# A hybrid encoder layer on one core: paired stick-breaking scores with masks on TensorE, later projection chunks, and sample memory attention in four column groups

## The chip, the cores and the metric

The kernel runs on one core of a Trainium2 chip. The metric is the device time of one execution in microseconds (us), the median of several runs. The engines are named as the profile names them: PE is TensorE (PEld its weight loads), DVE VectorE, ACT ScalarE, POOL GpSimd, SP the engine that issues most transfers.

## What is computed

One layer of a streaming encoder with the same weights for a prompt of 1024 frames and for 8 samples of 16 frames with 512 cached frames each. Model width 1024. Cut to what the change touches:

```python
def mla_attend(...):                    # 8 heads: latent keys, softmax over visible chunks
    ...
def stick_breaking_attend(q, k, v, q_pos, k_pos):      # 4 heads of 64
    z = jnp.einsum('bqhd,bkhd->bhqk', q, k) * SB_SCALE
    before = (k_pos[None, :] < q_pos[:, None])[None, None]
    log_beta = jax.nn.log_sigmoid(z)
    log_keep = jnp.where(before, jax.nn.log_sigmoid(-z), 0.0)
    between = lax.cumsum(log_keep, axis=3, reverse=True) - log_keep
    a = jnp.where(before, jnp.exp(log_beta + between), 0.0)
    return jnp.einsum('bhqk,bkhd->bqhd', a, v)

def memory_attend(x, mem_k, mem_v, g, w_q, w_o):       # 4 heads of 128, 256 memory tokens
    q = (rmsnorm(x, g) @ w_q).reshape(B, T, MEM_HEADS, MEM_HD)
    p = jax.nn.softmax(jnp.einsum('bqhd,bkhd->bhqk', q, mem_k) * MEM_SCALE, axis=-1)
    return jnp.einsum('bhqk,bkhd->bqhd', p, mem_v).reshape(B, T, -1) @ w_o

z = rmsnorm(x) @ w_in                   # split into MLA, retention and stick-breaking parts
mixed = concat([o_mla, ret_y, o_sb]);  x = x + mixed @ w_out
x = x + memory_attend(x, mem_k, mem_v, ...)            # each sample has its own mem_k, mem_v
x = x + conv_ffn(x, ...)                # up-projection, causal conv, SwiGLU, down-projection
```

The prompt's memory keys and values come from mem_prompt, each sample's from a cache.

## The kernel before

Activations lie feature-major: 128 features on the partitions, T = 1152 frames (1024 of the prompt, then 8 x 16 of the samples) in the free dimension. The matrices of weights are multiplied in three fp32r products (high part by high part, high by low, low by high), 128x384 each: one output block of 128 features is NCH = 3 chunks of 384 frames (split_products, L1864). POOL splits each 512 KB slot of weights into w_hi and w_lo (L813, L816). Attention works in f32, in which PE makes two passes of each matmul (two records in the profile).

In order of time the kernel has: input projection and retention (to about 300 us), one hand-written pipeline for stick-breaking and prompt MLA (to 640), sample MLA, the output projection W_OUT, memory queries, memory attention with its output (841 to 970), and the FFN (to the end).

**The pipeline of steps.** STEPS is a table. Five packs of query tiles, PACKS = (7), (6,0), (5,1), (4,2), (3), each of at most 1024 key columns per head, make one pass of two heads. Ten "sb" steps (t = 0 to 9, the first with tile 3) do the four stick-breaking heads of the prompt. Then come four pairs of prompt MLA heads of five "mla" steps each, with four "sbs" steps (sample stick-breaking, two samples each) among them. For each step t and head hh PE makes scores (scores, L2080; sample_scores, L2103) into the PSUM banks S[hh], then the transposes of step t-1 (L2129), then values of step t-2 (L2152). For sb steps DVE adds the mask `hide` to the diagonal blocks (sb_mask, L1509), ACT takes two sigmoids (sb_sigmoids, L986 and L987), DVE does a scan and a product (L1536, L1541), and ACT copies the transposed probabilities (probT, L1015). The two heads of an sb step lie on partitions 0 to 63 and 64 to 127 of z. For mla steps DVE takes the row maximum, ACT the exp (L1004), DVE the normalisation (L1552).

**Projection chunks.** STEP_CHUNKS (L270) says after which head of which step one of 11 chunks of the next MLA pair's q, k, v and absorbed q ("a") is projected (project_chunk, L2170 to L2182). PE puts it in bank 7. DVE evacuates q chunks (q_pass, L1575), ACT k, v and a chunks (L1059 to L1072). For the first pair they begin at step 2, two per step.

**Memory attention.** A loop over n = 0 to N_MEM+1 has eight prompt tiles (n = 0 to 7) and four pairs of samples (n = 8 to 11). PE makes scores of n, values of n-2 and transposes of n-1. For a pair of samples the scores use a 128-column weight qm_pair in which a sample's and head's 16 frames stand at their place among zeros, built by eight small ACT copies per pair (L1205): eight matmuls add up in one bank (L2329). Values take mv_c as weight and 16 columns of m_probT as moving operand, 16 matmuls per pair (sample_values, L2300), woven between the products of one of four early chunks of the memory output (memory_output, L2285). The other 20 of 24 chunks follow the loop, block by block; DVE adds each to x (L1737) and then does, per block m, the sums and split for the FFN's norm (residual, L1668, L1672, with ACT's square and rounding, L1158, L1159). x is reloaded by SP from x_mid in four transfers (L774). mk_c and mv_c are the samples' memory caches.

What releases whom is written by hand as semaphores; the functions that the change touches:

## Time and profile before

| | |
|---|---|
| median of 3 runs | 1822.57 us (1821.88 to 1822.60) |
| profiled execution | 1819.94 us |
| its span, first to last instruction | 1818.2 us |
| mean granted clock of PE | 0.985 |
| PE busy | 1760.5 us, 97% of the span |
| PEld busy | 1609.5 us, 89% |
| DVE busy | 1085.4 us, 60% |
| ACT busy | 538.9 us, 30% |
| POOL busy | 493.7 us, 27% |

The page gives, for the slowest core, each engine's busy time, the chain of work that ended last (followed back from the last instruction, at each step to what released it), the costliest groups, and the transfers. Windows give busy times in a stretch with the granted TensorE clock as a share of full speed: 1.00 is 2.4 GHz, 0.50 is 1.2 GHz. In a timeline, x6 at the end means six records in a row, and [3.80 <-DVE q_pass L1575] an idle time before them and what ended it. A matmul's end is modelled: the time to the next start is what counts in a stream.

### The profile page before, as it was taken

How to read it: one execution, taken by the hardware profiler on the slowest of the kernel's cores; microseconds unless marked ns; L12 is line 12 of the kernel's file. 1: busy time of each engine (PE TensorE's matmuls, PEld its weight loads, DVE VectorE, ACT ScalarE, POOL GpSimd, SP SyncE). 2: the span in 40 equal slices, each digit the busy share in tenths (PEclk: the TensorE clock that was granted, in tenths of full speed). 3: DMA queues.
4: the chain of work that ended last, by engine and by line, in shares of the span. 5: the costliest groups of instructions: out<-in, count | busy, mean ns of one | idle time of the engine just before them, and what ended most of it. 6: DMA issues, size and time to landing. Idle time of an engine off the chain costs nothing.

```text
span 1818.2 us, 26442 instructions
## 1 busy us (share of the span) xinstructions
PE 1760.5 (97%) x10471; PEld 1609.5 (89%) x10471; DVE 1085.4 (60%) x1459; ACT 538.9 (30%) x977; POOL 493.7 (27%) x219
## 2 busy tenths in 40 slices
PE   7999999899999999999999999999999999999997
PEld 7998799565666659998999999999999999999987
DVE  7864466676555745545446765655656556565667
ACT  6211211566555533112323312112121130211234
POOL 1771121000000102432023443333333433333331
PEclk9999999899999999999979999999999999999999
DMA  5230110411111402423321111111111111111112
GB/s 216 82 104 31 62 44 16 128 45 47 59 47 48 157 12 89 151 74 147 126 84 36 47 37 45 46 35 46 46 35 46 38 43 46 38 42 46 36 43 105
DMA packets 34973, 119.28 MB, mean 66 GB/s; under 512 B 4944, under 2 KB 7984, under 8 KB 32464
## 3 DMA queue, kind: packets, MB, share of 16 engines
q1 hardware_dynamic: 32592, 108.76, 18.5%
q10 hardware_dynamic: 2304, 9.44, 1.5%
q8 instruction: 56, 0.92, 0.2%
q14 instruction: 21, 0.17, 0.0%
HBM read 100.73 MB, written 15.17 MB: 64 GB/s over the span
## 4 chain that ended last, share of the span: by engine, by line
PE 89%; DVE 5%; ACT 2%; issue 2%; SPq 1%; DMA 1%; ACTq 0%; DVEq 0%
PE scores L1864 34%; PE bank L1864 32%; PE scores L2099 3%; PE bank L2129 2%; PE scores L1944 2%; PE bank L2152 2%; PE bank L2170 2%; PE scores L1888 1%; DVE kbuf L1536 1%; PE bank L2146 1%; PE bank L1875 1%; PE scores L2096 1%; PE scores L2329 1%; PE scores L2112 1%; PE bank L2300 1%
## 5 line engine op out<-in xcount | busy, mean ns | idle before, releaser
L813 POOL TENSOR_TENSOR w_hi<-w_raw,zero 128x1024 fp32r<-128x1024 f32 x96 | 188.9, 1968 | 1246.7 <-PE bank L1864 568.9
L1864 PE MATMUL scores<-act_hi,w_hi 128*128 128x384 f32 x960 | 324.2, 338 | 0.0
L1864 PE MATMUL scores<-act_hi,w_lo 128*128 128x384 f32 x960 | 322.6, 336 | 0.0
L1864 PE MATMUL scores<-act_lo,w_hi 128*128 128x384 f32 x960 | 322.6, 336 | 0.0
L816 POOL TENSOR_TENSOR w_lo<-w_raw,w_hi 128x1024 fp32r<-128x1024 f32 x96 | 251.2, 2617 | 7.6
L1792 DVE TENSOR_TENSOR x<-bank,x 128x384 f32<-128x384 f32 x216 | 120.4, 558 | 103.6 <-PE bank L1864 103.6
L1864 PEld LDWEIGHTS scores<-act_hi,w_hi 128*128 128x128 f32 x960 | 180.5, 188 | 0.6 <-issue 0.2
L1864 PEld LDWEIGHTS scores<-act_lo,w_hi 128*128 128x128 f32 x960 | 180.5, 188 | 0.3 <-issue 0.2
L1864 PEld LDWEIGHTS scores<-act_hi,w_lo 128*128 128x128 f32 x960 | 180.5, 188 | 0.0
L1864 PE MATMUL bank<-act_hi,w_hi 128*128 128x384 f32 x528 | 177.9, 337 | 0.0
L1864 PE MATMUL bank<-act_hi,w_lo 128*128 128x384 f32 x528 | 177.4, 336 | 0.0
L1864 PE MATMUL bank<-act_lo,w_hi 128*128 128x384 f32 x528 | 177.4, 336 | 0.0
L1766 DVE SCALAR_TENSOR_TENSOR conv<-ext,consts,conv 128x1168 f32<-128x1168 f32 x44 | 117.6, 2672 | 79.4 <-ACT conv L1231 79.4
L1864 PE MATMUL bank<-s_hi,w_hi 128*128 128x384 f32 (+2 forms) x454 | 153.0, 337 | 0.0
L1864 PE MATMUL bank<-s_lo,w_hi 128*128 128x384 f32 (+2 forms) x454 | 152.7, 336 | 0.0
L1864 PE MATMUL bank<-s_hi,w_lo 128*128 128x384 f32 (+2 forms) x454 | 152.6, 336 | 0.0
L1242 ACT ACTIVATE s_hi<-conv 128x1024 fp32r<-128x1024 f32 x20 | 21.2, 1060 | 344.1 <-DVE conv L1775 344.1
L1864 PEld LDWEIGHTS bank<-act_hi,w_hi 128*128 128x128 f32 x528 | 99.3, 188 | 1.0 <-issue 0.8
L1864 PEld LDWEIGHTS bank<-act_lo,w_hi 128*128 128x128 f32 x528 | 99.3, 188 | 0.0
L1864 PEld LDWEIGHTS bank<-act_hi,w_lo 128*128 128x128 f32 x528 | 99.3, 188 | 0.0
L1768 DVE SCALAR_TENSOR_TENSOR conv<-ext,consts,conv 128x1168 f32<-128x1168 f32 x44 | 84.3, 1916 | 5.7 <-DVE conv L1766 3.0
L1864 PEld LDWEIGHTS bank<-s_hi,w_hi 128*128 128x128 f32 x454 | 85.4, 188 | 0.4
(341 smaller groups left out, 3298.6 us busy)
## 6 DMA issues: line engine op xcount, KB each, us to landing
w_raw<-wstream SPq DMA_DIRECT2D x108, 512.0 KB, 3.6
x_blk<-xT ACTq DMA_DIRECT2D x8, 576.0 KB, 4.6
x_mid<-x_blk ACTq DMA_DIRECT2D x8, 576.0 KB, 3.1
x<-x_mid SPq DMA_DIRECT2D x4, 1152.0 KB, 7.8
z<-cache_k SPq DMA_DIRECT2D x4, 1024.0 KB, 5.3
z<-cache_v SPq DMA_DIRECT2D x4, 1024.0 KB, 7.3
mk_c<-mk_c SPq DMA_DIRECT2D x4, 1024.0 KB, 11.5
mv_c<-mv_c SPq DMA_DIRECT2D x4, 1024.0 KB, 13.5
```

What stands on the lines that cost most here:

```text
L813: pool.tensor_tensor(w_hi[:, k], w_raw[:, k], zero[:].unsqueeze(2).to_broadcast([P, KB, P]), ALU.add).then_inc(w_rounded, 1)
L816: pool.tensor_tensor(w_lo[:, k], w_raw[:, k], w_hi[:, k].bitcast(F32), ALU.subtract).then_inc(w_split, 1)
L1242: act.activation(dst[:, 0:TP], conv[:, 0, 0:TP], ACT.Copy)
L1766: own_v(dve.scalar_tensor_tensor(c, ext[:, ab, 1:EXT - 1], conv_tap(m + NFF * ab, 1), c, ALU.mult, ALU.add))
L1768: dve.scalar_tensor_tensor(c, ext[:, ab, 2:EXT], conv_tap(m + NFF * ab, 2), c, ALU.mult, ALU.add).then_inc(conv_done, 1)
L1792: dve.tensor_tensor(x[:, m, frames(c)], bank[6 + q % 2][:, 0:CH], x[:, m, frames(c)], ALU.add).then_inc(d_evac, 1)
L1864: mm = pe.matmul(out, w[:, k, at + kb], x(kb), start=first and kb == 0 and n == 0, stop=last and kb == n_kb - 1 and n == 2)
L1944: mm = pe.matmul(bank[c][:, 0:CH], w[:, 0, kb], x[:, kb, frames(c)], start=i == 0 and n == 0, stop=i == KB - 1 and n == 2)
L2099: mm = pe.matmul(S[hh][:, at:end], q_pass[i % 2][:, hh, tile(j)], k_pass[i % 2][:, hh, keys], start=True, stop=True)
L2129: mm = pe.transpose(bank[4 + g % 2][:, tile(b)], taken(t, hh)[:, tile(4 * k + b)], ident[:])
L2152: mm = pe.matmul(bank[6][64 * hh:64 * hh + 64, tile(n)], v, probT[:, t % 2, hh, at + P * b:at + P * b + P], start=b == 0, stop=b == j)
L2170: mm = pe.matmul(bank[7][:, 0:CH], w_pass[:, s, (2 * hh + kb) * P:(2 * hh + kb + 1) * P], z[:, Z_CQ + kb, frames(k)], start=kb == 0, stop= ...
```

## The change

- **Stick-breaking scores.** sb_scores(t) makes both heads' scores, piece by piece alternating head 0 (rows 0 to 63) and head 1 (rows 64 to 127), after both heads' previous sigmoids. After each tile PE adds the mask to the diagonal block of each head, as ident times hide accumulated in the bank. sb_mask on DVE is gone; ACT's sigmoids wait for s_ready and run ahead of the copies of probT. PE's order in an sb step is: scores of both heads, transposes of head 0, chunk, values, transposes of head 1, chunk.
- **Chunks of the first pair** follow the table FIRST_CHUNKS, from step 3 to step 9.
- **MLA.** A pair's first scores wait for the last k chunk, its first values for the last v chunk. ACT evacuates the chunk after head 1 before that head's exp.
- **sample_scores** alternates the two 64-column groups, f outside.
- **POOL** waits for the last prompt normalisation before it splits the W_OUT slots.
- **Sample memory attention.** Weights have 32 columns, head h writes partitions 32h to 32h+31 (scores into S[n%2], values into bank 6, with mv_c as moving operand of 128 columns). ACT copies the raw values (m_raw), PE turns them with two transposes into bank 7, ACT rounds and DVE splits. qm_pair is built once, at n = 4, by two ACT operations.
- **Memory output.** Seven chunks (MO_EARLY) are made inside the loop, at n = 8 to 14, in two banks, and DVE adds them there. The order of the 24 is new, with the third chunks of blocks 0 to 3 after the first two of each. SP issues the reloads of x in another order and earlier.

The diff, cut:

```diff
-MO_CHUNKS = [(0, 1), (1, 0), (0, 0), (1, 1)]
-MO_CHUNKS += [(m, c) for m in range(KB) for c in range(NCH) if (m, c) not in MO_CHUNKS]
+MO_CHUNKS = [(0, 0), (1, 0), (0, 1), (1, 1), (2, 0), (2, 1), (3, 0), (3, 1)] + [(m, 2) for m in range(4)]
+MO_CHUNKS += [(m, c) for m in range(4, KB) for c in range(NCH)]
+MO_EARLY = 7
+
+MO_BANKS = [(1, 3)[d % 2] if d < 8 else 3 * (m % 2) + c for d, (m, c) in enumerate(MO_CHUNKS)]
...
+FIRST_CHUNKS = ((3, 0), (3, 1), (4, 0), (4, 1), (5, 0), (5, 1), (6, 0), (6, 1), (7, 0), (9, 0), (9, 1))
+LAST_KEYS, LAST_VALUES = CHUNKS.index(("k", 1)), CHUNKS.index(("v", 1))
 STEP_CHUNKS = [[[], [], []] for _ in range(N_STEPS + 2)]
 for _n in range(NCK):
-    STEP_CHUNKS[2 + _n // 2][_n % 2 + 1].append((0, _n))
+    STEP_CHUNKS[FIRST_CHUNKS[_n][0]][FIRST_CHUNKS[_n][1]].append((0, _n))
...
-            for n in range(4):
-                if n < 2:
-                    sp.wait_ge(ms_ready, N_MEM)
-                else:
-                    sp.wait_ge(m_pv, N_MEM)
+            for n, through, count in ((0, ms_ready, NTILE), (1, qm_pair_ready, 1), (3, ms_ready, N_MEM),
+                                      (2, m_turned, DB // 2)):
+                if n == 0:
+                    sp.wait_ge(qm_pair_ready, 1)
+                sp.wait_ge(through, count)
                 sp.dma_start(x[:, 2 * n:2 * n + 2], io["x_mid"][:, 2 * n:2 * n + 2]).then_inc(x_in_again[n], 16)
...
+            pool.wait_ge(p_ready, N_ITEMS)
+            with pool.Fori(W_OUT // 2, NW // 2 - 1) as i:
...
             def sb_sigmoids(t, hh):
...
-                act.wait_ge(sb_masked, RANK[t][hh] + 1)
+                act.wait_ge(s_ready, ITEM[t][hh] + 1)
...
+                    if kind == "sb":
+                        sb_sigmoids(t, hh)
                     if 1 <= t <= N_STEPS and hh < n_heads(t - 1):
                         copy_groups(t - 1, hh)
-                    if t < N_STEPS and hh < n_heads(t):
-                        kind = STEPS[t][0]
-                        sb_sigmoids(t, hh) if kind == "sb" else sample_sigmoids(t) if kind == "sbs" else mla_exp(t, hh)
-                    for chunk in STEP_CHUNKS[t][hh]:
-                        evacuate_chunk(*chunk)
+                    if hh:
+                        for chunk in STEP_CHUNKS[t][1]:
+                            evacuate_chunk(*chunk)
+                    if kind == "mla":
+                        mla_exp(t, hh)
+                    elif kind == "sbs" and hh == 0:
+                        sample_sigmoids(t)
+                    if hh == 0:
+                        for chunk in STEP_CHUNKS[t][0]:
+                            evacuate_chunk(*chunk)
...
+                if NTILE <= n - 2 < N_MEM:
+                    c = n - 2
+                    act.wait_ge(m_pv, c + 1)
+                    if c >= NTILE + 2:
+                        act.wait_ge(m_turned, c - NTILE - 1)
+                    act.activation(m_raw(c), bank[6][:, 0:256], ACT.Copy).then_inc(m_raw_copied, 1)
...
-            def sb_mask(t, hh):
...
+                if n - 3 >= NTILE:
+                    split_output(n - 3)
+                if 0 <= n - NTILE < MO_EARLY:
+                    memory_residual(n - NTILE)
+
+            for d in range(MO_EARLY, len(MO_CHUNKS)):
+                memory_residual(d)
+                m, c = MO_CHUNKS[d]
+                if c == NCH - 1:
+                    residual(m, 2 * KB, x[:, m], "g_ffn")
...
+            def sb_scores(t):
+
+
+                _, i, tiles = STEPS[t]
+                for hh in range(2):
+                    if PREVIOUS[t][hh] is not None:
+                        pe.wait_ge(exp_done, PREVIOUS[t][hh] + 1)
+                for j, first, width in spans(t):
+                    for at, end in pieces(first, width):
+                        for hh in range(2):
+                            rows = slice(64 * hh, 64 * hh + 64)
+                            pe.matmul(S[hh][:, at:end], z[rows, Z_SQ + i, tile(j)],
+                                      z[rows, Z_SK + i, at - first:end - first], start=True, stop=True)
+                    for hh in range(2):
+                        mm = pe.matmul(S[hh][:, first + width - P:first + width], ident[:], hide[:], start=False, stop=True,
+                                       skip_group_check=True)
+                        if j == tiles[-1]:
+                            mm.then_inc(s_ready, 1)
...
-                for bb in range(2):
-                    rows = slice(64 * bb, 64 * bb + 64)
-                    for f in range(2):
-                        pe.matmul(S[0][rows, 0:PAST], sb_rows[:, 2 * p + bb, f], cache_k[:, bb, f], start=f == 0,
-                                  stop=f == 1)
...
+                for f in range(2):
+                    for bb in range(2):
+                        pe.matmul(S[0][64 * bb:64 * bb + 64, 0:PAST], sb_rows[:, 2 * p + bb, f], cache_k[:, bb, f],
+                                  start=f == 0, stop=f == 1)
...
+            for t in range(2, N_SB):
+                sb_scores(t)
+                transposes(t - 1, 0)
+                for chunk in STEP_CHUNKS[t][0]:
+                    project_chunk(*chunk)
+                values(t - 2)
+                transposes(t - 1, 1)
+                for chunk in STEP_CHUNKS[t][1]:
+                    project_chunk(*chunk)
...
+            def sample_memory_scores(n):
...
+                for bb in range(2):
+                    for h in range(GH):
+                        mm = pe.matmul(S[n % 2][32 * h:32 * h + 32, 0:MEM], qm_pair[:, p, bb, h], mk_c[:, p, bb, h],
+                                       start=bb == 0, stop=bb == 1)
+                mm.then_inc(ms_ready, 1)
+
+            def sample_memory_values(c):
...
+                for bb in range(2):
+                    for k in range(2):
+                        for h in range(GH):
+                            mm = pe.matmul(bank[6][32 * h:32 * h + 32, tile(bb)],
+                                           m_probT[:, 2 * (c % 2) + k, 32 * h:32 * h + 32],
+                                           mv_c[:, p, bb, k, tile(h)], start=k == 0, stop=k == 1)
+                mm.then_inc(m_pv, 1)
+
+            def turn_memory_values(c):
+                pe.wait_ge(m_raw_copied, c - NTILE + 1)
+                pe.wait_ge(om_split, c)
+                for bb in range(2):
+                    mm = pe.transpose(bank[7][:, tile(bb)], m_raw(c)[:, tile(bb)], ident[:])
+                mm.then_inc(m_turned, 1)
...
+                if n - 3 >= NTILE:
+                    turn_memory_values(n - 3)
+                if 0 <= n - NTILE < MO_EARLY:
+                    memory_output(n - NTILE)
+                if 2 <= n < N_MEM + 2:
```

Where instructions now stand. PE, the scores of step 3 (tiles 5 and 1; scores0 and scores1 are the banks of head 0 and head 1, z holds queries and keys, prob the probabilities of step 2), before:

```order
L2096 MATMUL scores0<-z_66 128x512
L2096 MATMUL scores0<-z_66 128x256 x2
L2129 MATMUL bank4<-ident_53,prob_93 128x128 x4
L2129 MATMUL bank5<-ident_53,prob_93 128x128 x4
L2096 MATMUL scores1<-z_66 128x512
L2096 MATMUL scores1<-z_66 128x256 x2
L2129 MATMUL bank4<-ident_53,prob_93 128x128 x4
L2129 MATMUL bank5<-ident_53,prob_93 128x128 x4
L2170 MATMUL bank7<-z_66,w_pass_108 128x384 x2
```

And after, from the second piece of tile 5 on:

```order
L2162 MATMUL scores0<-z_66 128x256
L2162 MATMUL scores1<-z_66 128x256
L2165 MATMUL scores0<-hide_110,ident_53 128x128
L2165 MATMUL scores1<-hide_110,ident_53 128x128
L2162 MATMUL scores0<-z_66 128x256
L2162 MATMUL scores1<-z_66 128x256
L2165 MATMUL scores0<-hide_110,ident_53 128x128
L2165 MATMUL scores1<-hide_110,ident_53 128x128
L2196 MATMUL bank4<-ident_53,prob_93 128x128 x4
L2196 MATMUL bank5<-ident_53,prob_93 128x128 x4
L2239 MATMUL bank7<-z_66,w_pass_108 128x384 x2
L2221 MATMUL bank6<-probT_100,sv_tok_76 64x128 x16
```

Both heads' scores now stand ahead of all transposes, the two heads' matmuls alternate, a mask follows each tile, and the second head's transposes stand behind the values.

PE in the memory loop, n = 10 (mk_c and mv_c are the samples' caches, om_hi and om_lo the attention output, split), before:

```order
L2329 MATMUL scores0<-mk_c_139,qm_pair_138 128x256 x8
L1864 MATMUL scores0<-om_hi_134,w_hi_50 128x384
L2300 MATMUL bank6<-m_probT_137,mv_c_140 128x16 x2
L1864 MATMUL scores0<-om_lo_135,w_hi_50 128x384
L2300 MATMUL bank6<-m_probT_137,mv_c_140 128x16 x2
```

And after, from the end of n = 9 to the scores of n = 11:

```order
L2449 MATMUL bank4<-ident_53,m_prob_136 128x128
L2449 MATMUL bank5<-ident_53,m_prob_136 128x128
L2380 MATMUL scores0<-mk_c_139,qm_pair_138 32x256 x8
L1918 MATMUL scores0<-om_hi_134,w_hi_50 128x384
L1918 MATMUL scores0<-om_lo_135,w_hi_50 128x384
L1918 MATMUL scores0<-om_hi_134,w_lo_51 128x384
```

On PE then come the other nine products of this chunk, and behind them, up to the chunk of n = 11:

```order
L2394 MATMUL bank6<-mv_c_140,m_probT_137 32x128 x16
L2449 MATMUL bank4<-ident_53,m_prob_136 128x128
L2449 MATMUL bank5<-ident_53,m_prob_136 128x128
L2380 MATMUL scores1<-mk_c_139,qm_pair_138 32x256 x8
L2403 MATMUL bank7<-ident_53,m_probT_137 128x128 x2
```

The values stand in one piece behind a whole output chunk instead of between its products, and the two turning transposes are new.

## Rows read from the trace of the kernel before

**Rows 1.** The page's chain that ended last, shares of the span by engine.
```profile
PE 89%; DVE 5%; ACT 2%; issue 2%; SPq 1%; DMA 1%; ACTq 0%; DVEq 0%
```

**Rows 2.** Windows: us, busy us (instructions) of each engine, TensorE clock, DMA share, GB/s.
```profile
340.50:357.50 17.00, 16.47 (x40) 9.20 (x42) 10.45 (x14) 7.24 (x10) 0.00 (x0) 0.50 0.01 3
360.00:410.00 50.00, 47.70 (x334) 31.64 (x334) 37.87 (x46) 35.70 (x64) 0.00 (x0) 1.00 0.16 41
637.40:640.90 3.50, 3.13 (x24) 2.81 (x26) 2.83 (x8) 1.79 (x5) 0.00 (x0) 0.51 0.36 130
...
910.50:931.00 20.50, 19.84 (x76) 19.02 (x77) 1.78 (x5) 0.72 (x3) 0.00 (x0) 0.50 0.18 65
```

**Rows 3.** Timeline of PE: start, us, engine, line, operation, passes, idle before.
```profile
341.03 2.08 PE L2173 MATMUL bank<-z,w_pass 128*128 128x512 f32 x2 [3.80 <-DVE q_pass L1575]
...
418.86 1.55 PE L2099 MATMUL scores<-k_pass,q_pass 128*128 128x512 f32 x3
```

**Rows 4.** Timeline of step 7, PE and ACT.
```profile
395.40 1.09 PE L2129 MATMUL bank<-ident,prob 128*128 128x128 f32 x8
...
396.43 1.99 PE L2096 MATMUL scores<-z 64*128 64x512 f32 x6
...
397.07 1.03 ACT L986 ACTIVATE kbuf<-scores 128x1024 f32<-128x1024 f32 x1
...
399.04 1.08 ACT L1015 ACTIVATE probT<-bank 128x512 f32<-128x512 f32 x2
...
400.00 1.97 PE L2152 MATMUL bank<-probT,sv_tok 128*64 128x128 f32 x32
```

**Rows 5.** Timeline of PE, step 0.
```profile
298.67 1.13 PE L2096 MATMUL scores<-z 64*128 64x512 f32 x4
```

**Rows 6.** Timeline of PE, retention.
```profile
160.07 0.49 PE L2035 MATMUL bank<-q_dec,state 128*128 128x128 f32 x2
160.49 0.44 PE L2032 MATMUL bank<-kept,rv_tok 128*64 128x128 f32 x4
```

**Rows 7.** Waits of PE from 418 to 625: us in total, times, longest.
```profile
PE bank L2170 <- ACT k_pass L1060: 4.3, 3, 1.4
```

**Rows 8.** Timeline of PE, the first sample stick-breaking step.
```profile
449.34 1.93 PE L2112 MATMUL scores<-z,sb_rows 128*64 128x512 f32 x4
...
451.12 0.64 PE L2112 MATMUL scores<-z,sb_rows 128*64 128x512 f32 x1
451.22 0.49 PE L2115 MATMUL scores<-z,sb_rows 128*64 128x128 f32 x3
...
453.41 0.76 PE L2129 MATMUL bank<-ident,prob 128*128 128x128 f32 x5
```

**Rows 9.** Timeline of DVE and POOL in prompt MLA.
```profile
434.99 0.88 DVE L1552 TENSOR_SCALAR prob<-prob,row_sum 128x896 f32<-128x896 f32 x2
...
628.07 3.68 DVE L1552 TENSOR_SCALAR prob<-prob,row_sum 128x640 f32<-128x640 f32 x2
...
633.58 2.47 POOL L816 TENSOR_TENSOR w_lo<-w_raw,w_hi 128x1024 fp32r<-128x1024 f32 x1
```

**Rows 10.** Waits of PE from 600 to 645.
```profile
PE bank L2129 <- DVE prob L1552: 4.0, 2, 2.4
PE bank L2129 <- DVE probT L1562: 0.8, 1, 0.8
```

**Rows 11.** Timeline of PE, memory attention and its outputs.
```profile
876.14 3.62 PE L2329 MATMUL scores<-mk_c,qm_pair 128*128 128x256 f32 x16
...
930.90 0.38 PE L1864 MATMUL bank<-om_hi,w_hi 128*128 128x384 f32 x1
...
933.02 0.34 PE L1864 MATMUL scores<-om_hi,w_hi 128*128 128x384 f32 x1
...
970.47 0.34 PE L1944 MATMUL scores<-act_hi,w_hi 128*128 128x384 f32 x1
```

**Rows 12.** Groups of DVE from 875 to 971: busy, mean ns, idle before.
```profile
L1668 DVE TENSOR_TENSOR sumsq<-sumsq,square 128x1152 f32<-128x1152 f32 x6 | 9.6, 1605 | 7.4 <-ACT square L1158 7.4
```

222 lines of the change are left out of this document (107 added, 115 removed).

## The prediction

> **What bounds the kernel now.** I read the page's chain of waits first: TensorE (PE) holds 89% of the chain that ends last, DVE 5% [rows 1]. So time is won where PE works at half clock, where it waits, or where it does work that can run beside other work. The windows by stage [rows 2] show both of the first two: 340.5 to 357.5 at a granted clock of 0.50 (1.2 GHz) in the stick-breaking steps, 637.4 to 640.9 at 0.51 at the end of prompt MLA, 910.5 to 931 at 0.50 in memory attention, and the clean stretch 360 to 410 at 1.00 with PE busy 47.7 of 50 us. The timeline of PE [rows 3] shows what stood ahead of the first: an idle 3.80 us at 341.03, where a k chunk waits for DVE's q_pass. Times below are against the profiled execution, 1819.94 us (its span is 1818.2). The median of the runs is 1822.57, 0.14% above.
>
> **Part 1, stick-breaking scores, masks and chunks.** Step 7 shows what a step costs PE [rows 4]: scores 1.99 a head (1.91 to the next start, the rest is the modelled end), transposes 1.03 a head, values 1.97 (1.90 to the next start); two projection chunks are about 2.5 more. Scores of one head are 1024 columns in two passes, and use 64 rows of the array. The change puts the two heads next to each other on rows 0 to 63 and 64 to 127. The trace has that once, at step 0: four passes of 512 columns, two of each head, in 1.13 us [rows 5], where 2048 columns of one head take 1.91. So both heads cost 1.91 to 2.3 instead of 3.82. Added are the masks on PE: two tiles x two heads x two passes of 128 columns, 8 x 0.11 = 0.9, and changes between 64-row and 128-row work. For such a change I take the nearest row, the retention products that alternate between 64-column and 128-column weights: two passes begin at 160.07 and the next group at 160.49, 0.42 us for 0.22 of columns (eight transposes of 128 are 1.03 with a change, so 0.11 each), so 0.1 to 0.2 each [rows 6]. Four of them are 0.4 to 0.8. I take 3.2 us for both heads with masks; the ends are 2.8 and 4.0.
>
> The Trainium skill, TensorEngine Tiling (Array Packing), section Key Properties, says that a change of the tiling mode drains TensorE; it speaks against these masks and gives no price. The 0.2 us gaps of rows 6 agree with it.
>
> A step with two chunks then has 3.2 + 2.06 + 1.9 + 2.5 = 9.6 us of PE. A step without is not bound by PE (7.2) but by the loop that both heads' sigmoids close: scores 3.2, sigmoids of head 0 1.95, the two copies of probT 1.08, sigmoids of head 1 1.95, some 0.5 of releases: 8.7 (the two ACT rows start 1.97 apart [rows 4]). Step 2 cannot begin before head 1 of step 1 is through its sigmoids; with both heads' scores of step 1 done near 324 and DVE's product of step 0 as last release, I place it at 330.2, some 2 later than now. Going on: 338.6, 348.2, 357.8, 366.7, 376.3, 384.9, 393.4, and the first MLA step at 401. Before, that one began at 418.86 [rows 3]. That is 17.9 gained, less 0.5 for the masks at step 0: 17.4. The stall goes because the first k chunk now comes in step 3, behind a q chunk whose q_pass no longer waits for the transfer that held it. Of the 17.4, some 8.5 is the half clock (17.0 us at half speed), 3.8 the stall, 5 the paired scores. What is late next is the sigmoid loop. It leaves PE idle near 329 and 337, and an idle stretch of this kind is what stood ahead of every half-clock stretch in rows 2 and 3, so I take off 2: **15.5**. Ends 7 (clock falls, see below) and 19. The masks that leave DVE (0.43 each) give nothing of their own: DVE's scan and product, 3.6 us per head, fit in the step. PE's new wait for the mask's transfer, ahead of step 0 near 298, costs nothing, since DVE's wait for the same transfer ended no chain before; were it late, step 0 and the last input blocks would stand behind it.
>
> **Part 2, MLA.** PE waited three times, 4.3 us in all, for the k_pass evacuation that stood behind the exps on ACT, at chunk matmuls [rows 7]. ACT now evacuates before exp(t,1), and a pair's first step waits only for keys. The exp is 0.5 to 1 us later for it, and PE has work between. I take **2.5**; ends 0 and 4.3.
>
> **Part 3, sample stick-breaking scores.** Four steps of 449.34 to 453.41, 4.07 us each: the two 64-column groups run one after the other. But the groups overlap where they meet [rows 8]: a 512-column pass of the second group starts at 451.12, ahead of the last three short passes of the first, at 451.22. So alternated they share the time: 4 x 0.44 (449.34 to 451.12 is four passes) + 4 x 0.11 = 2.2, against 4.07, 1.9 a step, 7.6 in all, of which up to 1 comes back as waits for the sigmoid behind it: **6.5**, ends 0 and 7.6.
>
> **Part 4, Pool's splits of the W_OUT slots.** Four operations, the last of them the Pool row in [rows 9], ran up to 636.05 beside DVE's normalisations: 3.68 us for two where two of more columns take 0.88. PE waited 4.0 us for these [rows 10] and 0.8 for a copy behind them, then worked 3.5 us at half clock (1.7). The change holds them until the last prompt normalisation (near 640), and their first use is near 688, 40 us later, for 9 us of work. Beside them run then the first operations of sample MLA, the first on DVE at 650. **6.2**, less 0 to 2 if they now meet sample MLA.
>
> The Trainium skill, SBUF — State Buffer, section SBUF: two separate sides, calls the port pair of VectorE and GpSimd an exclusive lock that fully blocks the loser. By it a normalisation that meets a split waits for the whole split. The row at 628.07 agrees, two in 3.68 us beside Pool operations of up to 2.47.
>
> **Part 5, sample memory attention.** Before, from 876.14 to 970.47 [rows 11] lie 94.3 us: four sample scores of 3.62, four outputs with 16-column values woven in, and 20 plain outputs, of which one is 930.90 to 933.02 (2.12 with the clock's rise ahead of it, 2.08 steady). 20.5 us of it at half clock, 10.2 lost. Now, by iteration: n=8 has sample scores (16 passes of 256 columns, 0.22 each, over four column groups: 0.9), an output 2.08, prompt values 1.95 and transposes 1.03 (as rows 4): 6.0. n=9: 0.9 + 2.08 + 1.95 + 0.22 = 5.15. n=10: values of the sample are 32 passes of 0.11 over four groups, 0.9: 4.1. n=11: 4.3 with the two turning transposes. n=12 3.4, n=13 3.2, n=14 2.3. Sum 28.4, plus 1.6 for changes of mode (8 x 0.2) and 1.5 where a turn or a value waits for ACT's copy: 31.5. Then 17 outputs, 35.4. DVE now gets the sums of rows 0 to 3 in a burst, since their third chunks come last: 3.9 to 4.6 us each (square and two DVE operations, of which one is 1.6 in the mean [rows 12] and grows when Pool splits beside it) against 2.08 of PE. PE waits about 1 for bank 5, and DVE ends 43 to 49 us after the early outputs, where the first FFN block wants the last row at 47.4: I take 3.2 in all, ends 1 and 8. Column groups of 32 never overlap in this trace, so I add 1.5 for overlap that is less than whole, and 1.4 for DVE's seven early sums ahead of the softmax. 73.0 in all, FFN at 949.1 instead of 970.5: **21.4**, ends 12 and 26. The reload of x, issued at 7 prompt tiles instead of after the loop, comes behind mk_c and mv_c on SP; it is due at n=8 and may hold DVE for a us. Half clock is absent because no thin 16-column stretch is left.
>
> **Sum.** 15.5 + 2.5 + 6.5 + 6.2 + 21.4 = 52.1, so 1767.8 for a profiled execution and, 0.14% higher, **1770** for the median.
>
> **Rivals.**
> A, column groups share only two at a time. If the two passes of a matmul must run one behind the other before the next matmul's first, at most two groups are ever busy: 4 x 0.9 more for scores and as much for values, 7 us: 1777. The row at 451.12 in rows 8 speaks against it (a pass of a later matmul starts ahead of earlier passes), and so do rows 5, where both heads' four passes fit in 1.13 us. Chance 0.12. The Trainium skill, TensorE: Matmul & The Clock Gate, Part 3, has matmuls start and end strictly in program order; it would give this rival, and rows 8 do not fit it pass by pass.
> B, the half clock stays in stick-breaking. PE idles near 329 and 337 waiting for sigmoids, after transposes with little else; a stretch like that of 17 us costs 8.5, of which 2 are in the sum: 1777. For it: every half-clock stretch here stands behind or in thin work. Chance 0.2. With A: 1784, 0.03.
> C, the change does not do what it says: the heads' rows do not overlap once masks stand between them. 8 steps of 1024 columns a head x 1.9 = 15: 1785. Rows 5 speak against it. Chance 0.03.
> D, the burst: DVE's sums with Pool splits beside all of them hold the FFN's first block 8 instead of 3, and the SP reload holds DVE: 1776. Chance 0.08, within the range.
> E, slower. Work on parts of the array keeps the clock at its lower level from step 1 until it ends: stick-breaking (73 us of PE work) and the memory loop (31.5) twice as long. That adds 104.5 to 1770, less the 2 already counted: about 1872. It decides when more than 104 us stand at half clock, since a stretch costs half its length and the gain is 52. Against it: 360 to 410, with 64-row scores and 64-column values throughout, is at 1.00 [rows 2]. Chance 0.01.
>
> **Chances and range.** My forecast (1760 to 1775) has 0.5, A 0.12, B 0.2, A with B 0.03, C 0.03, D 0.08, E 0.01, and 0.03 for more gain than the sum (parts at their better ends: 1756). The range 1757 to 1788 takes in all but part of C, E and some of the last; it holds the part-by-part ends with several of them bad at once (Part 1 at 7 and Part 5 at 15 is 1785). About 0.2% is what this measurement can tell from no change: faster 0.98, same 0.01, slower 0.01.
>
> **What would show it.** Right: windows at 340, 637 and 910 at clock 1.00; pairs of score passes with starts a few ns apart, 3.2 us a step; step periods of 9.6 with chunks and 8.7 without; first MLA step near 401; sample scores of 2.2; normalisations at 0.9 a pair near 625 and no PE wait there; memory scores and values of about 1 us each; FFN near 918 in the new count (949 less the 31 gained earlier). Wrong: a wait for exp at each step's start over 1 us; any half-clock stretch over 5 us before 930; memory scores of 1.8; a wait of the first FFN block for act_lo.

## The result and the profile after

The changed kernel takes 1765.47 us (median of 4 runs, 1764.60 to 1766.45), beside 1822.22 for the kernel before: a ratio of 0.9689, 95% interval 0.9672 to 0.9706. The forecast was 1770, the range 1757 to 1788. The medians are 56.8 us apart, the two profiled executions 53.5: that of the kernel before (1819.94) lay 2.3 under its median, that of the change (1766.45) 1.0 over its own.

From the page of the profiled execution (1766.45 us, span 1764.6), the busy times and the chain that ended last, to set beside [rows 1]:

```profile
PE 1716.0 (97%) x10543; PEld 1577.6 (89%) x10543; DVE 1074.6 (61%) x1439; ACT 537.1 (30%) x951; POOL 493.1 (28%) x219
...
PE 90%; DVE 4%; ACT 3%; issue 2%; DMA 1%; ACTq 0%; SPq 0%; DVEq 0%
```

PE is as busy a share of a shorter span. The windows of the change by stage, in the columns of [rows 2]:

```profile
200.70:207.50 6.80, 6.80 (x33) 5.57 (x33) 0.00 (x0) 1.81 (x3) 0.00 (x0) 0.61 0.01 2
332.70:342.40 9.70, 9.66 (x44) 6.70 (x44) 5.13 (x3) 4.05 (x6) 0.00 (x0) 0.52 1.01 346
342.40:392.40 50.00, 49.87 (x405) 35.37 (x404) 44.88 (x50) 40.05 (x70) 0.00 (x0) 1.00 0.15 35
603.00:620.00 17.00, 16.00 (x147) 10.67 (x143) 7.75 (x20) 7.48 (x21) 8.45 (x4) 1.00 0.12 34
842.80:915.20 72.40, 66.80 (x537) 60.57 (x537) 41.09 (x60) 23.23 (x44) 15.49 (x6) 1.00 0.25 88
```

In the stick-breaking steps the half clock has not gone, it has shrunk and moved: 9.7 us at 0.52 from 332.7, where before it was 17.0 us at 0.50 from 340.5. Behind it, from 342.4 to 392.4, PE is busy 49.87 of 50 us. Between 603 and 620, the end of prompt MLA, and in the whole of the memory part the clock is 1.00. The first row is a stretch that no part of the change touches, and is read further down.

The timeline of PE (start, us, engine, line, operation, records, idle before) at steps 2 to 4:

```profile
332.74 3.36 PE L2162 MATMUL scores<-z 64*128 64x512 f32 x8 [2.45 <-ACT prob L1029]
...
343.64 1.56 PE L2162 MATMUL scores<-z 64*128 64x512 f32 x8
...
346.95 1.04 PE L2196 MATMUL bank<-ident,prob 128*128 128x128 f32 x8
...
351.11 1.09 PE L2196 MATMUL bank<-ident,prob 128*128 128x128 f32 x8
352.04 1.02 PE L2242 MATMUL bank<-z,w_pass 128*128 128x512 f32 x2
352.99 1.35 PE L2162 MATMUL scores<-z 64*128 64x512 f32 x8
```

and at the first MLA step, which [rows 3] had at 418.86:

```profile
404.39 1.98 PE L2142 MATMUL scores<-k_pass,q_pass 128*128 128x512 f32 x4
```

Both heads' scores of step 3 with their masks take 343.64 to 346.95, 3.31 us; two heads of before took 3.82 without masks. Steps with two chunks are 9.35 us apart. PE stands 2.45 us for the sigmoids ahead of step 2, and the half clock begins right there.

The waits of PE in MLA (total, times, longest), beside [rows 7], and the timeline of the first sample stick-breaking step, beside [rows 8]:

```profile
PE bank L2239 <- ACT v_pass L1106: 1.0, 1, 1.0
...
PE bank L2239 <- ACT k_pass L1102: 0.5, 2, 0.3
```

```profile
433.70 1.94 PE L2178 MATMUL scores<-z,sb_rows 128*64 128x512 f32 x8
435.47 0.61 PE L2182 MATMUL scores<-z,sb_rows 128*64 128x128 f32 x8
436.00 1.09 PE L2196 MATMUL bank<-ident,prob 128*128 128x128 f32 x8
```

The three waits for k_pass, 4.3 us, are now two of 0.5 in all, and a sample step's scores take 2.30 us instead of 4.07. The memory part, beside [rows 11]: the timeline of PE, and its waits from 840 to 930.

```profile
842.80 1.07 PE L2380 MATMUL scores<-mk_c,qm_pair 128*32 128x256 f32 x16
...
857.33 1.08 PE L2394 MATMUL bank<-mv_c,m_probT 128*32 128x128 f32 x32
858.34 0.44 PE L2449 MATMUL bank<-ident,m_prob 128*128 128x128 f32 x2
```

```profile
915.23 0.34 PE L1996 MATMUL scores<-act_hi,w_hi 128*128 128x384 f32 x1
...
927.50 0.45 PE L1996 MATMUL scores<-act_hi,w_hi 128*128 128x384 f32 x1 [1.18 <-DVE act_lo L1716]
```

```profile
PE bank L1918 <- DVE x L1753: 2.1, 1, 2.1
PE bank L2403 <- DVE om_lo L1742: 1.9, 2, 1.2
PE scores L1996 <- DVE act_lo L1716: 1.2, 1, 1.2
PE scores L1918 <- DVE x L1753: 1.1, 2, 0.6
```

Scores of a pair of samples are 1.07 us (3.62 before), values 1.08. New are three waits for DVE's adds of x (2.1 and 1.1 us), two for its om_lo (1.9) and one for its act_lo (1.2).

Where the time went, by starts of PE's instructions in the two timelines (the stretches add up to the spans, 53.6 us apart):

| stretch | before | after | gain | forecast |
|---|---|---|---|---|
| start to scores of step 1 | 320.73 | 323.41 | -2.7 | 0 |
| to first MLA scores | 98.13 | 80.98 | 17.1 | 15.5 |
| to sample MLA | 228.17 | 210.82 | 17.4 | 15.2 |
| to sample memory scores | 229.11 | 227.59 | 1.5 | 0 |
| to FFN | 94.33 | 72.43 | 21.9 | 21.4 |
| to the end | 847.73 | 849.37 | -1.6 | 0 |

Of the 2.7 us lost ahead of step 1, 0.4 are the masks at step 0: from its scores to those of step 1 it is 22.50 us, and 22.06 before. The prediction charged 0.5 for them, in its Part 1. The rest is variation, read at the end.

### The profile page after: what moved, and what is told of

Read it like the earlier page. It is cut to its first block, busy times and chain, and to the rows that moved or that the text cites. A ratio compares the mean times of both kernels' runs of the same rounds, so it can differ in the third digit from the quotient of the medians.

```text
span 1764.6 us, 26569 instructions
## 1 busy us (share of the span) xinstructions
PE 1716.0 (97%) x10543; PEld 1577.6 (89%) x10543; DVE 1074.6 (61%) x1439; ACT 537.1 (30%) x951; POOL 493.1 (28%) x219
## 4 chain that ended last, share of the span: by engine, by line
PE 90%; DVE 4%; ACT 3%; issue 2%; DMA 1%; ACTq 0%; SPq 0%; DVEq 0%
PE scores L1918 33%; PE bank L1918 32%; PE scores L2142 3%; PE bank L2196 3%; PE bank L2221 2%; PE bank L2239 2%; PE scores L1996 1%; PE scores L2162 1%; PE scores L1940 1%; PE bank L2215 1%; PE bank L1927 1%; PE scores L2310 1%; PE scores L2165 1%; PE scores L2309 1%; ACT square L1208 1%
## 5 line engine op out<-in xcount | busy, mean ns | idle before, releaser
L1295 ACT ACTIVATE s_hi<-conv 128x1024 fp32r<-128x1024 f32 x20 | 21.2, 1060 | 344.1 <-DVE conv L1829 344.1
## 6 DMA issues: line engine op xcount, KB each, us to landing
mv_c<-mv_c SPq DMA_DIRECT2D x4, 1024.0 KB, 14.8
```

Source lines behind the costliest of these rows:

```text
L1295: act.activation(dst[:, 0:TP], conv[:, 0, 0:TP], ACT.Copy)
```

## The experiments

Each run is read by its stretches, from its profiled execution, since the first one varies by itself. How long PE is at half clock in a stretch also differs between runs whose instructions there are the same; where this bears on a reading, it is said. The last column of this table says how the median of the whole came out.

| run | step 1 to MLA | MLA to sample MLA | memory to FFN | median |
|---|---|---|---|---|
| before | 98.1 | 228.2 | 94.3 | 1822 |
| the change | 81.0 | 210.8 | 72.4 | 1765.5 |
| before, later chunks | 87.7 | 228.5 | 94.3 | 1809.5 |
| before, POOL's wait | 100.4 | 221.2 | 94.3 | 1814.1 |
| before, samples alternated | 98.3 | 222.5 | 99.2 | 1818.3 |
| change, heads in turn | 81.5 | 210.9 | 72.5 | 1764.8 |
| change, heads apart | 91.8 | 210.9 | 73.5 | 1774.9 |
| change, masks on DVE | 88.2 | 210.2 | 72.4 | 1771.7 |
| change, exp first | 81.4 | 214.8 | 72.4 | 1768.6 |
| change, groups in turn | 81.0 | 210.9 | 79.0 | 1771.0 |
| change, four early | 81.0 | 210.9 | 72.4 | 1765.4 |
| change, tail order | 81.0 | 211.0 | 70.8 | 1764.6 |
| change, sigmoids first | 77.6 | 210.9 | 72.4 | 1760.2 |
| both last ideas | 77.6 | 210.8 | 71.2 | 1759.1 |

### How much the pairing gives: heads in turn, heads apart

```diff
-                    for at, end in pieces(first, width):
-                        for hh in range(2):
+                    for hh in range(2):
+                        for at, end in pieces(first, width):
```

> The change with one edit: within a tile all pieces of head 0, then all of head 1 (tiles 4 to 7 have two pieces of up to 512 columns; smaller tiles have one and stay alternated). Same matmuls, same masks. Theory (row groups share time only where the two heads' matmuls stand next to each other): tiles 4 to 7 of steps 1 to 8 lose their overlap, 1.9 + 1.7 + 1.4 + 1.2 us twice, 12 in all, less some 0.4 at each border where the heads meet: the first MLA scores 9 to 12 us later than in the change, the median 1774 to 1777. Rival (the array starts a pass of a free row group however far down the queue it stands, or the steps are bound by sigmoids anyway): under 3 us later.

Measured: 81.5 us, 0.6 more than the change. The rival holds. Step 5, which has two pieces a head, from this run's timeline:

```profile
360.83 1.99 PE L2162 MATMUL scores<-z 64*128 64x512 f32 x8
```

Eight passes of 512 columns in 1.99, as in the change: four passes of head 0 stood ahead of four of head 1, and all ran in pairs. The 0.6 is not the order's. The run with the exp first (below) has the stick-breaking instructions of the change in the change's order, and is 0.5 longer too. Its windows:

```profile
330.30:333.70 3.40, 3.17 (x8) 1.27 (x8) 3.24 (x2) 0.58 (x2) 0.00 (x0) 0.50 1.02 220
333.70:340.50 6.80, 5.05 (x48) 4.13 (x48) 3.40 (x4) 5.13 (x8) 0.00 (x0) 1.00 1.00 392
340.50:343.90 3.40, 3.40 (x12) 1.80 (x10) 3.37 (x5) 0.99 (x4) 0.00 (x0) 0.50 0.18 66
```

Heads in turn has the same two stretches at half clock, 330.5 to 333.9 and 340.7 to 344.1, where the change has one, 331.8 to 342.1. So 6.8 us at half clock cost this stretch a little more than 10.2 did. With the clock at 1.00 in the middle, PE waits 0.49 us for probT and 1.26 for the sigmoids of step 3; the change, slower there, has neither wait. Of the 4.9 us of PE's work that the half clock cost the change, these 1.75 would have been waits anyway: some 3 is my estimate of what it cost the stretch.

```diff
...
-                sb_scores(t)
+                sb_scores(t, (0,))
                 transposes(t - 1, 0)
+                sb_scores(t, (1,))
```

> The change with the transposes of head 0 between the two heads' scores from step 2 on, as the kernel before had them; masks on PE, chunks, all else as the change. Theory (eight transposes of 128 rows between them are too far to look ahead and use all rows): each head's scores cost 1.9 us more on PE in seven steps of 1024 columns a head and 1 in step 9; steps that PE bounds (five with two chunks, one with one) get longer by it, the others hardly: the stretch from the scores of step 1 to the first MLA scores 10 to 14 us longer than the 81.0 of the change. Rival (head 0's sigmoids start earlier, so the loop gives most back): under 6 us.

Measured: 91.8 us, 10.8 more; the theory holds. Step 3 in this run's timeline:

```profile
340.93 1.55 PE L2162 MATMUL scores<-z 64*128 64x512 f32 x4
342.41 0.49 PE L2165 MATMUL scores<-hide,ident 128*128 128x128 f32 x2
...
344.75 1.55 PE L2162 MATMUL scores<-z 64*128 64x512 f32 x4
```

The score passes of one head take 1.55 us, which is what those of both heads took together (1.56 at 343.64 in the change). In this run PE never waited 2.45 us ahead of step 2, and had no half clock there (clock 1.00 from 320 to 360), so the two ends of the stretch are read apart. From the scores of step 1 to those of step 3 it is 4.0 us shorter than the change (16.2 against 20.2). From there to the first MLA scores, where both runs are at clock 1.00, it is 14.8 longer (75.5 against 60.7), and this is what the pairing is worth in these steps. The medians differ by 9.4. The profiled execution (1782.04) was the longest of this run's four, the others took 1774.3 to 1774.9; only its stick-breaking stretch is used here.

### Masks on DVE

The change with sb_mask back, its wait and call as in the kernel before:

```diff
-                        mm = pe.matmul(S[hh][:, first + width - P:first + width], ident[:], hide[:], start=False, ...)
...
+                dve.tensor_tensor(last, last, hide[:].unsqueeze(1).to_broadcast([P, len(STEPS[t][2]), P]),
+                                  ALU.add).then_inc(sb_masked, 1)
```

> The change with the masks back on DVE (added to the diagonal blocks before the sigmoids), scores of both heads still alternated. Each tile's masks cost PE 0.6 us in the profile of the change (354.27 to 354.91), 1.2 us in a two-tile step. Theory (DVE is the next bound): scans 4.6, products 2.6, two masks 0.9 and a q chunk 0.6 to 1.1 are about 9.0 us of DVE, against the change's 9.4 us step, so the steps shrink by 0.4 and the first MLA scores come about 3 us earlier. Rival 1 (masks on PE pay, as the sigmoids wait for nothing on DVE): 2 to 6 us later. Rival 2 (PE alone bounds): 8 us earlier.

Measured: 88.2 us, 7.2 longer, with as much at half clock as in the change (10.2 us); the median is 1771.67 us. My theory had the wrong sign, and rival 1 was right with a larger size. Waits of PE from 295 to 406, and the timeline around step 6 in this run:

```profile
PE bank L2203 <- ACT probT L1057: 11.3, 7, 2.6
PE scores L2172 <- ACT prob L1029: 7.8, 8, 2.4
```

```profile
370.48 2.00 PE L2172 MATMUL scores<-z 64*128 64x512 f32 x12 [0.36 <-ACT prob L1029]
...
373.34 1.22 DVE L1594 TENSOR_TENSOR prob<-prob,kbuf 128x1023 f32<-128x1023 f32 x1
...
374.48 0.42 DVE L1562 TENSOR_TENSOR scores<-scores,hide 128x256 f32<-128x256 f32 x1
...
374.94 1.02 ACT L1028 ACTIVATE kbuf<-scores 128x1024 f32<-128x1024 f32 x1 [2.41 <-DVE scores L1562]
```

The scores of step 6 start at 370.48, done near 372.4, but the sigmoid begins at 374.94: DVE works in order, and its mask waits behind the product of the step before (373.34). DVE has time enough for the masks; it has it too late. PE then waits 11.3 us for probT and 7.8 for sigmoids; in the change it waits 3.4 for sigmoids and not at all for probT.

### Later chunks alone

The kernel before, with this edit only:

```diff
+FIRST_CHUNKS = ((3, 0), (3, 1), (4, 0), (4, 1), (5, 0), (5, 1), (6, 0), (6, 1), (7, 0), (9, 0), (9, 1))
-    STEP_CHUNKS[2 + _n // 2][_n % 2 + 1].append((0, _n))
+    STEP_CHUNKS[FIRST_CHUNKS[_n][0]][FIRST_CHUNKS[_n][1]].append((0, _n))
```

> The kernel before with only the table of the first pair's chunks changed (from step 3 on, as in the change). Theory (the stall of 3.8 us at 341 and the half clock behind it, 8.5 us, come from the early q chunk that waits for a transfer): both go, other waits stay; the first MLA scores 10 to 13 us earlier than before, median 1809 to 1813. Rival (the half clock comes from the thin work around the sigmoids at step 2, as it does in the change from 332.7 to 342.4): only 4 to 8 us earlier, with a half-clock stretch near 330.

Measured: 10.4 us less in the stretch; ratio to before 0.9927 (0.9912 to 0.9943). A window of this run:

```profile
336.00:350.00 14.00, 12.13 (x67) 7.51 (x68) 12.69 (x15) 9.25 (x16) 0.00 (x0) 0.88 0.33 130
```

The stall of 3.80 is gone, and of 17 us at half clock there is little left (0.88 over 14 us, which is 3.4 at half).

### POOL's wait, samples alternated, exp first

Three edits, each the one of the change put into the kernel before, or taken back in the change:

```diff
+            pool.wait_ge(p_ready, N_ITEMS)
```

> The kernel before with only POOL's wait for the last prompt normalisation ahead of the W_OUT slots. Theory: the waits of PE at 631.8, 636.3 and 637.8 (4.8 us) and the half clock behind them (1.7) go: 6.5 us faster, median 1815.7, normalisations of two in 0.9 us throughout. Rival (the contention moves to sample MLA's normalisations, or W_OUT's first slot comes late): under 3 us faster.

Measured: 7.0 us less from MLA to sample MLA (221.2), no wait of PE for a normalisation between 600 and 645, and nothing given back behind it (228.9 to the memory scores, 229.1 before). Ratio 0.9951 (0.9935 to 0.9968). The 100.4 us of the first stretch, 2.3 more than before, are not the edit's: this run has 6.8 us at half clock from 412.5, among instructions that the edit leaves alone.

```diff
-                for bb in range(2):
...
-                    for f in range(2):
...
+                for f in range(2):
+                    for bb in range(2):
...
```

> The kernel before with only the sample stick-breaking scores alternating between the two 64-column groups. Before, eight passes of one group stand ahead of the other's. Theory (passes overlap with a free group's only when few passes stand between, as heads in turn with four passes each cost nothing and values in turn with eight cost 1.4 us a pair): 2.3 us a step instead of 4.07, four steps, 7 us less from the first MLA scores to sample MLA (228.2 in the profile before, so 221). Rival (the steps were bound by the sigmoids behind them): under 3 us.

Measured: 222.5, 5.7 us less; the theory holds. The scores of a step take 2.31 us (448.55 to 450.86), 7.0 less over four steps. The last 1.4 of it are lost again at the end of prompt MLA, where this run has 6.8 us at half clock from 629.1 and the kernel before had 3.4 from 637.4. In the memory part, which the edit leaves alone, it has 30.7 us at half clock instead of 20.5, and takes 99.2 us instead of 94.3; no run shows why. Its ten runs lie between 1810 and 1822, ratio 0.9973 (0.9959 to 0.9988), so the median says less than the stretch.

```diff
-                    if hh:
-                        for chunk in STEP_CHUNKS[t][1]:
-                            evacuate_chunk(*chunk)
                     if kind == "mla":
                         mla_exp(t, hh)
...
-                    if hh == 0:
-                        for chunk in STEP_CHUNKS[t][0]:
-                            evacuate_chunk(*chunk)
+                    for chunk in STEP_CHUNKS[t][hh]:
+                        evacuate_chunk(*chunk)
```

> The change with ACT's old order in MLA steps: the exp of head 1 ahead of the chunk that is evacuated after head 1. Theory: three waits of PE for k_pass come back, 4.3 instead of 0.5 us: 3.8 us slower. Rival (with the pair's first scores waiting for keys alone, or with other slack, the waits are covered): under 1 us.

Measured: 4.0 us more in MLA, with the three waits for k_pass back at 4.3. Together 7.0 + 5.7 + 4.0 = 16.7 of the 17.4 that this stretch gained (18.1 with the 1.4 of half clock named above).

### Memory groups in turn, four early chunks, another order

```diff
-                for bb in range(2):
-                    for h in range(GH):
+                for h in range(GH):
+                    for bb in range(2):
                         mm = pe.matmul(S[n % 2][32 * h:32 * h + 32, 0:MEM], ...
```

and the same for the values.

> The change with one edit: the sample memory scores and values go head by head, so that successive matmuls use the same 32-column group and move to the next only after two (scores) or four (values). Theory (groups share time only when they alternate): scores of a pair 3.5 us instead of 1.0, values 3.5 instead of 1.0, four pairs: 20 us slower than the change less borders, some 15 to 20, with the clock at 1.00 because outputs stand between. Rival 1 (the queue starts passes of free groups ahead): under 3 us slower. Rival 2 (work on 32 columns at a time brings the clock down): over 25 us slower with half-clock stretches near 850.

Measured: 6.5 us more, between theory and rival 1. The timeline of PE in this run:

```profile
843.04 1.09 PE L2380 MATMUL scores<-mk_c,qm_pair 128*32 128x256 f32 x16
...
857.62 2.46 PE L2394 MATMUL bank<-mv_c,m_probT 128*32 128x128 f32 x32
860.02 0.44 PE L2449 MATMUL bank<-ident,m_prob 128*128 128x128 f32 x2
```

The scores, with four passes for each group, cost 1.09 (1.07 in the change). The values, with eight passes for each group, cost 2.46 instead of 1.08: 4 x 1.4 = 5.5. The other 1.0 goes with a half-clock stretch of 3.4 us from 892.0, which the change does not have. So how far ahead a free group starts is a matter of passes. The starts of the single records from 857.62 on show it: one pass every 0.11 us, then, from the fifth (858.09) on, two at a time, which is the second group beside the first, and so on for each next group. By this count four groups of eight take 3 x 4 + 8 = 20 passes of 0.11, an estimate of 2.2 us and the start. In [rows 8] the second group started with the fifth of eight passes as well (451.12, ahead of the last three).

```diff
-MO_EARLY = 7
+MO_EARLY = 4
```

> The change with four instead of seven memory output chunks inside the loop. Theory (the last iterations, n = 12 to 14, have nothing but turns, values and waits for ACT and DVE without a chunk, and the three chunks come later in full): 3 to 5 us longer from the first sample memory scores to the FFN (72.4 in the change). Rival (DVE's burst of sums sets the end of this part, and three more chunks for PE behind the loop only fill its waits): under 1.5 us.

Measured: 72.43, the same to the hundredth. The theory is wrong, and so is the reason that the rival gives. The timeline of this run at n = 12:

```profile
861.50 0.41 PE L2403 MATMUL bank<-ident,m_probT 128*128 128x128 f32 x2 [1.20 <-DVE om_lo L1742]
```

PE waits 1.20 for om_lo, as in the change (1.21, at 864.82), because the turning transposes stand ahead of the chunk there: the three chunks covered nothing. Nor did they fill waits behind the loop: those for DVE's adds are 2.1 and 1.1 us, as in the change. Whether the first four chunks help is not tested.

```diff
-MO_CHUNKS = [..., (3, 0), (3, 1)] + [(m, 2) for m in range(4)]
+MO_CHUNKS = [..., (3, 0), (0, 2), (1, 2), (3, 1), (2, 2), (3, 2)]
```

> The change with another order of the memory output chunks: the third chunks of blocks 0 and 1 directly after the seven early ones, then (3,1), then the third chunks of blocks 2 and 3. Theory (PE's waits of 2.1 and 1.1 us for DVE's adds and 1.2 us for act_lo in the first FFN block come from DVE's burst of sums): DVE starts its burst a chunk earlier and PE has one chunk more to do in it; 1.5 to 3 us faster. Rival (the burst is bound by DVE with POOL's splits beside it, whatever PE's order): no difference, or slower by a wait for the last samples' split ahead of the first third chunk.

Measured: 1.6 us less to the FFN, at the low end of the theory: PE's waits for DVE's adds fall from 3.2 us to 1.6. The wait for act_lo in the first FFN block stays 1.2. The last stretch is 2.4 longer (851.7 against 849.3), but not by DVE's burst: the FFN runs as in the change for its first 784 us, to within 0.02, and the 2.4 arise at its end, where this run is at half clock in these two windows and the change from 1707.4 to 1710.8 only:

```profile
1701.50:1708.30 6.80, 5.46 (x13) 4.30 (x14) 1.98 (x3) 1.25 (x2) 0.00 (x1) 0.50 0.00 0
1739.10:1742.50 3.40, 3.15 (x10) 2.55 (x11) 0.53 (x2) 1.96 (x5) 0.00 (x0) 0.50 0.83 308
```

So the stretch supports the theory and not the rival. The median, 1764.56, is not told apart from the change's.

### Two versions that go further

ACT at step 1, and PE's scores of step 2 ahead of the last value transposes:

```diff
             sb_sigmoids(1, 0)
+            sb_sigmoids(1, 1)
             stick_breaking_values(0)
...
-            sb_sigmoids(1, 1)
...
+            sb_scores(2)
             pe.wait_ge(sv_copied["act"], 2)
             value_tokens(4)
...
-                sb_scores(t)
+                if t > 2:
+                    sb_scores(t)
```

> The change with the start of the stick-breaking steps in another order: ACT takes both heads' sigmoids of step 1 before any copy, and PE makes the scores of step 2 ahead of the last value transposes and the transposes of step 0. Theory (the half clock from 332.7 to 342.4 follows the thin stretch 327.8 to 332.7, in which PE works 1.3 of 5 us): PE idles some 2.3 instead of 3.7 us and the half clock does not come: 1.4 + 4.9 = 6 us faster, median 1759.5. Rival (an idle stretch of 2 us is enough for the half clock): 1 to 2 us faster and half clock from about 330.

Measured: 1760.22 us, ratio to before 0.9661 (0.9648 to 0.9675); the stretch is 77.6, 3.4 less. The windows, and the timeline of PE at step 2:

```profile
322.00:337.00 15.00, 10.35 (x84) 7.94 (x83) 11.21 (x9) 10.89 (x16) 0.00 (x0) 1.00 1.01 310
337.00:345.00 8.00, 7.99 (x69) 5.82 (x70) 7.90 (x10) 5.91 (x10) 0.00 (x0) 1.00 0.33 121
```

```profile
326.69 1.77 PE L2162 MATMUL scores<-z 64*128 64x512 f32 x8 [2.14 <-ACT prob L1029]
328.39 0.71 PE L2165 MATMUL scores<-hide,ident 128*128 128x128 f32 x4
```

PE still waits 2.14 us for sigmoids, but has work close before and behind, and the clock stays at 1.00. The theory holds for the clock; of its 6 us the stretch gives 3.4, because PE's waits between the scores of step 1 and of step 3 grow from 3.7 to 4.7 us (step 3 alone waits 1.26 for sigmoids).

The second version has this edit and, in the memory loop, one more:

```diff
-                if n - 3 >= NTILE:
+                if n - 3 >= NTILE and n not in (N_MEM, N_MEM + 1):
                     turn_memory_values(n - 3)
                 if 0 <= n - NTILE < MO_EARLY:
                     memory_output(n - NTILE)
+                if n in (N_MEM, N_MEM + 1):
+                    turn_memory_values(n - 3)
```

> The run with both heads' sigmoids of step 1 first (1760.2 us), and in iterations 12 and 13 of the memory loop the output chunk ahead of the turning transposes, so that PE no longer waits 1.2 and 0.7 us for DVE's split of the pair before. Theory: 1.5 to 2 us less in the memory part, median 1758 to 1759. Rival (DVE's burst behind the loop sets the end): no difference to 1760.2.

Measured: 1.25 us less in the memory part, 1759.09 us, 0.9658 (0.9639 to 0.9677). At the turning transposes 2.2 us are gained, and 3.4 us at half clock from 879.3, which the first version does not have, take part of it back. The stretch supports the theory; the medians of the two versions are not told apart by these intervals. Every run of either is shorter than every run of the change.

## Why the prediction was right

The whole came closer than its parts: the stretches missed by +1.6, +2.2, +1.5, +0.5, -2.7 and -1.6 us, which partly cancel, and that is luck. What the parts rest on, step by step:

**Part 1.** The sum said 15.5 (17.4 less 2 is 15.4), the stretch gave 17.1. Step 2 was placed at 330.2; it began at 332.74, or at 330.06 without the 2.7 us by which step 1 came late. Steps with two chunks and two tiles took 9.35 to 9.39 us instead of 9.6, since each head's transposes come cheaper (0.87 from 346.95 to 347.82, 0.93 from 351.11 to 352.04) than the 1.03 that I charged twice. Scores with masks were 3.31 for 3.2. Rival B came true in part: 9.7 us at half clock and 4.9 of PE's work lost, some 3 of them in the stretch by the estimate above, where the sum held 2. The wait ahead of it, 2.45 us, was foreseen: step 2 was placed some 2 later than before because it waits for both heads' sigmoids.
Two statements of this part failed although the sum held. "5 the paired scores" was too low: apart, the heads cost 10.8 us more over the stretch, and 14.8 in the part that both runs have at full clock. I had set off the masks on PE against the pairing and called the rest "pairing". And "the masks that leave DVE give nothing of their own" was wrong by 7.2 us. It may hold for the kernel before, where no run tests it, but with both heads' scores done at once a mask on DVE stands behind the scan and product of the other head. I had counted DVE's load and not its order.
Later chunks alone give 10.4 of the 17.1, the stall and most of the half clock. The other 6.7 need pairing and masks together, as the table shows: 87.7 us with later chunks alone, 88.2 with paired heads but masks on DVE, 91.8 with masks on PE but heads apart, 81.0 with both. The last three also have the new order of ACT (sigmoids ahead of the copies of probT), which no run tests by itself, and each of the four has its own half clock (3.4, 10.2, 0 and 10.2 us).

**Part 2.** 2.5 forecast, 4.0 measured: the waits fell by 3.8, and the exp that now comes later cost nothing.

**Part 3.** 6.5 forecast, 5.7 measured alone (7.1 without the longer half clock of that run); a step's scores take 2.30 for the 2.2 worked out.

**Part 4.** 6.2 forecast, 7.0 measured. No contention moved to sample MLA.

**Missing from the sum.** The 1.5 us between sample MLA and the memory scores: eight small ACT copies for each pair of samples are now two in all, and PE's waits for ACT's m_probT fell from 2.2 to 1.3 us. That the one caused the other is argued, no run tests it. The part on memory did not price work taken from ACT. The 1.6 us lost in the last stretch is mostly the wait of 1.2 for act_lo in the first FFN block, 1.5 from start to start; the forecast had it inside Part 5.

**Part 5.** 21.4 forecast, 21.9 measured; the loop from 842.80 to 875.73 took 32.9 for 31.5 plus 1.4, the rest 39.5 for 35.4 plus 3.2, with waits of 2.1 and 1.1 for DVE's adds where 1 to 8 was allowed. The 1.5 set aside for overlap that is less than whole was not needed. What the part had wrong is that all seven early chunks help: four or seven of them make no difference. By the rows, four sample scores of 1.07 instead of 3.62 are 10.2 us and the half clock that is gone 10.2. No run puts the column groups alone into the kernel before, so that the thin 16-column values brought the half clock is argued from where it stood. The prediction's reading that an idle stretch stood ahead of every half-clock stretch does not hold there: ahead of 910.5 PE was busy 33.97 of 34.40 us. Nor is the new memory part free of half clock in every run: three runs (heads apart, groups in turn, both last ideas) have 3.4 us of it within 2 us of the end of the 2.1 us wait for DVE's adds, while the change has that wait and none.

**Rivals.** A is refuted by 1.07 us for sixteen passes of 0.22. C is refuted. D did not come: DVE's adds and act_lo held PE 3.2 and 1.2 us, where it had 8 for the first FFN block. E did not come; 342.4 to 392.4 is all packed work at clock 1.00. Of the signs that the prediction named for being wrong, two came, the half-clock stretch of over 5 us and the wait for act_lo; the time stayed in the range with both.
The Trainium skill, TensorE: Matmul & The Clock Gate, Part 3, has matmuls in strict program order; heads in turn at 1.99 us for both show passes of a free row group that start ahead of earlier ones, and here the measurement decides.

## What to carry to other kernels

Price an operation by where it stands in its engine's order, not only by the engine's free time: masks of 0.4 us each, on an engine with time to spare, cost 7 us over ten steps. When a wait leaves PE thin, look at what the clock does behind it: with the sigmoids first, PE waits 1.0 us longer in sum than in the change, and the stretch is still 3.4 shorter, since its half clock is gone. And two edits can be worth nothing one by one and 6.7 us together, as pairing and masks on PE were here. Before work is put somewhere as cover, look whether the wait stands ahead of it.

## What the runs showed that I had not expected

**Alternation is not needed, closeness is.** Groups of rows or columns overlap when up to four passes of one group stand ahead of the other's (heads in turn 1.99 us, scores of samples in turn 1.09), in part with eight (2.46 for 1.08, and 4.07 for 2.30 in the sample steps), and not at all across eight transposes that use the whole array (1.55 us for each head).

**A stretch that no version changed varies.** The windows row at 200.7 to 207.5 of the change shows 0.61. The same window in the run with POOL's wait, whose instructions there are those of the kernel before:

```profile
200.70:207.50 6.80, 6.80 (x37) 4.69 (x37) 2.78 (x6) 3.79 (x3) 0.00 (x0) 1.00 0.00 0
```

Step 1 starts between 319.14 and 324.70 us over the runs, which is why parts of a few us are read here from stretches and not from medians.
